# A mixture of experts on one core: nine instead of eight buffers for the experts' weights

## What is computed

```python
scores = jax.nn.sigmoid(ht @ w_router)              # 256 tokens x 64 experts
... # eight experts are chosen for each token, in four of eight groups
combine = ...                                       # weight of each chosen expert
a = jnp.einsum('td,edf->tef', hb, w_gate)           # 1024 -> 256, each expert
u = jnp.einsum('td,edf->tef', hb, w_up)             # 1024 -> 256
routed = jnp.einsum('tef,efd->td', silu(a) * u * combine[..., None], w_down)
shared = (silu(ht @ ws_gate) * (ht @ ws_up)) @ ws_down
x = x + gt2 * (routed + shared)                     # x is the residual
```

## Time and profile before

| | us |
|---|---|
| median of 3 runs | 1518.18 (1514.33 to 1518.4) |
| profiled execution, its own time | 1515.46 |
| its span, first to last instruction | 1513.6 |
| PE busy | 1451.0 (96%) |
| DVE busy | 985.3 (65%) |
| ACT busy | 792.3 (52%) |

### The profile page before, as it was taken

How to read it: one execution, slowest core, us unless ns; L and a number is a source line. 1 busy time by engine, 2 the same in 40 slices (tenths; PEclk the granted TensorE clock), 3 DMA queues, 4 the chain that set the end, 5 groups by cost and what they waited for, 6 DMA issues and landing times.

```text
span 1513.6 us, 39194 instructions
## 1 busy us (share of the span) xinstructions
PE 1451.0 (96%) x16093; PEld 1182.4 (78%) x16093; DVE 985.3 (65%) x1383; ACT 792.3 (52%) x1015; POOL 96.5 (6%) x57
## 2 busy tenths in 40 slices
PE   7999899999999999999999999899999999999998
PEld 6997767999999989999898999775555555555554
DVE  3597433367665457754645645678887787888786
ACT  5446226344333359634234445456767666767674
POOL 1200300002432000000310000000000000000000
PEclk9999999999999999999999999999999999999999
DMA  9667277455555535543123345379998999998994
GB/s 299 187 203 226 81 240 252 170 164 184 172 191 177 188 112 167 167 140 112 59 92 133 117 129 179 144 312 380 410 414 354 415 396 411 415 412 357 415 415 185
DMA packets 178599, 362.32 MB, mean 239 GB/s; under 512 B 9229, under 2 KB 137722, under 8 KB 161658
## 3 DMA queue, kind: packets, MB, share of 16 engines
q1 hardware_dynamic: 178426, 359.90, 65.5%
HBM read 355.03 MB, written 1.05 MB: 235 GB/s over the span
## 4 chain that ended last, share of the span: by engine, by line
PE 73%; DVE 6%; DMA 4%; ACT 4%; issue 2%; DVEq 1%; ACTq 0%; SPq 0%; POOLq 0%
PE psum L3395 11%; PE psum L372 9%; PE psum L373 8%; PE psum L376 8%; PE psum L3411 6%; DMA proj<-in_w_exp_up 4%; PE psum L3366 3%; PE psum L3448 3%; PE psum L569 3%; PE psum L704 3%; PE psum L505 2%; PE psum L506 2%; PE psum L507 2%; PE psum L547 2%; PE psum L1191 1%
## 5 line engine op out<-in xcount | busy, mean ns | idle before, releaser
L372 PE MATMUL psum<-proj_r 128*128 128x256 f32 x1392 | 341.6, 286 | 3.9 <-ACT proj_r L336 3.9
L373 PE MATMUL psum<-proj_r 128*128 128x256 f32 x1392 | 339.1, 284 | 0.0
L341 DVE TENSOR_TENSOR ring_r<-ring,proj_r 128x2048 fp32r<-128x2048 f32 x94 | 223.6, 2380 | 156.9 <-ACT proj_r L336 156.2
L2585 DVE COPY ring<-proj 128x1024 f32 x374 | 237.0, 686 | 91.8 <-PE psum L3395 53.5
L372 PEld LDWEIGHTS psum<-proj_r 128*128 128x128 f32 x1392 | 268.0, 193 | 8.3 <-issue 7.3
L373 PEld LDWEIGHTS psum<-proj_r 128*128 128x128 f32 x1392 | 268.1, 193 | 0.1
L336 ACT ACTIVATE proj_r<-ring 128x2048 fp32r<-128x2048 f32 x93 | 177.5, 1908 | 103.6 <-PE psum L376 93.1
L1919 ACT ACTIVATE ring<-proj 128x1024 f32 x186 | 188.9, 1051 | 6.6 <-issue 5.4
L376 PE MATMUL psum<-proj_r,ring_r 128*128 128x256 f32 x1392 | 181.3, 283 | 0.0
L376 PEld LDWEIGHTS psum<-proj_r,ring_r 128*128 128x128 f32 x1392 | 173.3, 192 | 0.1
L3395 PE MATMUL psum<-ring,u 128*32 128x256 f32 x1488 | 114.8, 386 | 3.2 <-DVE ring L2585 2.4
(11 more groups left out here) (570 smaller groups left out, 2621.5 us busy)
## 6 DMA issues: line engine op xcount, KB each, us to landing
ring<-in_w_in SPq DMA_DIRECT2D x65, 1024.0 KB, 5.3
proj<-in_w_exp_gate SPq DMA_DIRECT2D x64, 1024.0 KB, 9.4
proj<-in_w_exp_up SPq DMA_DIRECT2D x64, 1024.0 KB, 10.0
proj<-in_w_exp_down SPq DMA_DIRECT2D x64, 1024.0 KB, 8.2
ring<-in_w_ada SPq DMA_DIRECT2D x24, 1024.0 KB, 8.2
ring<-in_w_ffn_in SPq DMA_DIRECT2D x22, 1024.0 KB, 5.1
ring<-in_w_ffn_out SPq DMA_DIRECT2D x11, 1024.0 KB, 4.9
ring<-in_w_out SPq DMA_DIRECT2D x8, 1024.0 KB, 5.1
```

The lines of the kernel that those rows point to most:

```text
L341: dve.tensor_tensor(ring_r[:, at.slot, :], ring[:, at.slot, :], self.heads[at.buffer].bitcast(F32), ALU.subtract) \
L372: pe.matmul(dst, w, xh, start=start, stop=False, skip_group_check=True)
L373: pe.matmul(dst, w, xl, start=False, stop=False, skip_group_check=True)
L2585: ins = dve.tensor_copy(into_copy[k_half][j][:, kind * D:(kind + 1) * D], pieces[:, bass.ds((piece + kind) & 7, 1), of_half].rearrange("p ...
```

## The change

The ring gets a ninth buffer, `proj[:, 64:72]`. The copy that lay there (the second block's gate and up, lower half of the contraction) moves to `delta`. The residual's token rows, which lay in `delta`, are written to the output tensor in HBM before the piece d0 is issued (two DMAs of 512 KB), and read back into a ring buffer after the last piece (two DMAs again), for the last sums. The first copy into `delta` waits for the write. A piece now waits for the one nine places earlier, which is the same matrix of the expert three before.

```diff
-        pieces = proj[:, 0:64, :].rearrange("p (r k) n -> p r (k n)", r=8)
+        pieces = proj[:, 0:8 * PIECES, :].rearrange("p (r k) n -> p r (k n)", r=PIECES)
-        into_slots = [ring[:, 1, :], ring[:, 2, :], ring[:, 3, :], flat_of(proj[:, 64:72, :])]
+        into_slots = [ring[:, 1, :], ring[:, 2, :], ring[:, 3, :], flat_of(delta[:, :, :])]
+        h_back = pieces[:, (3 * EXPERTS + 1) % PIECES, :].rearrange("p (b d) -> p b d", b=TB)
...
+            def spill_h_tok():
+                sp.wait_ge(*reached("last_h_copied", 1))
+                for b in range(TB):
+                    sp.dma_start(out[0, b * P:(b + 1) * P], h_tok[:, b, :]).then_inc(sig("h_kept"), 16)
             for at, e, kind in piece_order:
-                if at - 8 in at_place:
-                    last, kind_before = at_place[at - 8]
-                    if at == 8:
+                if at == 5:
+                    spill_h_tok()
+                if at - PIECES in at_place:
+                    last, kind_before = at_place[at - PIECES]
+                    if at == PIECES:
...
-                dst = pieces[:, (at + 1) % 8, :]
+                dst = pieces[:, (at + 1) % PIECES, :]
...
+            sp.wait_ge(*reached("h_kept", 32))
+            last = EXPERTS - PIECES // 3
+            ended = sp.value_load(ends_of[:, last:last + 1], min_val=1, max_val=BLOCKS)
+            sp.wait_ge(*reached("into_copied", ended * 2 + (ended & 1)))
+            for b in range(TB):
+                sp.dma_start(h_back[:, b, :], out[0, b * P:(b + 1) * P]).then_inc(sig("h_returned"), 16)
...
-                                          pieces[:, bass.ds((piece + kind) & 7, 1), of_half].rearrange("p o n -> p (o n)"))
+                                          pieces[:, bass.ds((piece + kind) % PIECES, 1), of_half].rearrange("p o n -> p (o n)"))
...
             for k_half in range(2):
+                if k_half:
+                    dve.wait_ge(*reached("h_kept", 32))
                 copy_into(0, k_half, 1, by_block[1])
...
                 dve.wait_ge(*reached("moe_scaled", 3 + b))
-                dve.tensor_tensor(out_tok[:, b, 512:D], out_tok[:, b, 512:D], h_tok[:, b, 512:D], ALU.add).then_inc(sig(f"out_ready_{b}_1"), 1)
+                dve.wait_ge(*reached("h_returned", 32))
+                dve.tensor_tensor(out_tok[:, b, 512:D], out_tok[:, b, 512:D], h_back[:, b, 512:D], ALU.add).then_inc(sig(f"out_ready_{b}_1"), 1)
```

More of the change, by code:

```diff
@@ L39 @@
 SLOTS = 6
+PIECES = 9
 SLOT = 2048
@@ L145 @@
     "state_written": [("state_ready", 3), ("g_state_ready", 3)],
+    "tiles_moved": [("input_heads_moved", 16), ("input_rests_moved", 16), ("h_kept", 32), ("h_returned", 32)],
     "logits_made": [("att_scored", 2), ("d_scored", 8)],
@@ L1391, in _ @@
                     dst = dst.rearrange("p (f n) -> p f n", f=2)
-                sp.dma_start(dst, src).then_inc(sig(f"piece_loaded_{at % 8}"), 16)
+                sp.dma_start(dst, src).then_inc(sig(f"piece_loaded_{at % PIECES}"), 16)
+            sp.wait_ge(*reached("h_kept", 32))
[4 more added lines that the diff above has]
+                sp.dma_start(h_back[:, b, :], out[0, b * P:(b + 1) * P]).then_inc(sig("h_returned"), 16)
             for b, n in ((0, 0), (1, 0), (1, 1), (0, 1)):
@@ L1450, in _ @@
                 pool.tensor_tensor(u[:, pair, :], h[:, pair, :], spread(rs[:, :], 2), ALU.mult).then_inc(sig("pair_scaled"), 1)
-            loads_before = [0] * 8
+            loads_before = [0] * PIECES
             places_passed = 0
             for at, e, kind in piece_order:
-                loads_before[at % 8] += 1
-                pool.wait_ge(*reached(f"piece_loaded_{at % 8}", 16 * loads_before[at % 8]))
+                loads_before[at % PIECES] += 1
+                pool.wait_ge(*reached(f"piece_loaded_{at % PIECES}", 16 * loads_before[at % PIECES]))
                 pool.drain().then_inc(sig("pieces_in"), at + 1 - places_passed)
@@ L1460, in _ @@
                 pool.wait_ge(*reached("moe_scaled", b + 1))
-                pool.tensor_tensor(out_tok[:, b, 0:512], out_tok[:, b, 0:512], h_tok[:, b, 0:512], ALU.add).then_inc(sig(f"out_ready_{b}_0"), 1)
+                pool.wait_ge(*reached("h_returned", 32))
+                pool.tensor_tensor(out_tok[:, b, 0:512], out_tok[:, b, 0:512], h_back[:, b, 0:512], ALU.add).then_inc(sig(f"out_ready_{b}_0"), 1)
             st.end()
@@ L1916, in down_of_block @@
                     act.wait_ge(sig("pieces_in"), piece + 5)
-                    down_from.append(pieces[:, bass.ds((piece + 5) & 7, 1), :])
+                    down_from.append(pieces[:, bass.ds((piece + 5) % PIECES, 1), :])
                 at = slice(part * D, (part + 1) * D)
@@ L2594, in down_of_last @@
                 dve.wait_ge(sig("pieces_in"), piece + 5)
-                dve.tensor_copy(last_down[j], pieces[:, bass.ds((piece + 5) & 7, 1), :].rearrange("p o n -> p (o n)")).then_inc(sig("last_down_copied"), 1)
+                dve.tensor_copy(last_down[j], pieces[:, bass.ds((piece + 5) % PIECES, 1), :].rearrange("p o n -> p (o n)")).then_inc(sig("last_down_copied"), 1)
             choose(0)
```

## The result

| | before | changed |
|---|---|---|
| median of 6 runs, us | 1518.29 | 1508.2 (1503.95 to 1511.79) |
| profiled execution, us | 1515.46 | 1507.84 |
| its span | 1513.6 | 1506.0 |

The ratio is 0.9942, with a 95% interval of 0.9924 to 0.9961: 8.8 us less, 5.9 to 11.5 (the medians themselves are 10.1 us apart). The forecast was 3.6 us less, 1514.6 us, with a range that reached down to 1508.0 us; the time came out 0.2 us inside its edge, where the first rival stood.

What follows compares the result with a forecast made beforehand. PE was taken to set the time in the experts' stage, with late weights costing at most 12.8 us. Terms -2.5 - 0.4 - 0.7 = -3.6 us gave 1514.6 us against the median; range 1508 to 1519.5 us.

Steps and rivals of the forecast that it cites:

- the first rival: Falls of the clock at both places go or get shorter: -7 us up to the whole 12.8 us, 1505.4 to 1511 us; chance 0.22.
- Term 3: PE's wait at 1254.88 us and the low clock behind it stay: 0, bounds -2.9 - 3.4 us and 0.
- Term 1: Expert 20: d21 goes out within the stall, so u23 and all pieces behind it land one piece earlier: -2.5 us.
- The clock at 1173 us: PE would otherwise wait for u24, so it gains the pieces' 2.5 us, without adding the clock fall's 1.7 us.
- Term 2: The wait ahead of expert 20 goes, since the stream of pieces gets ahead at the start: -0.4 us.
- Term 4: Wait at 1490.03 us, expert 60: last up piece comes at least one place earlier: -0.7 us, bounds 0 and 1.14 us.
- Term 5: Residual's write at the start lands by 993.2 us, before the copy needing it; the stream's 2 to 3 us lead is cover: 0.
- Term 6: Residual's read back behind d63, more than 10 us ahead of POOL's first last sum: 0; without cover, up to 4.9 us.
- Term 7: Register remainder ahead of each copy, mostly done while the copy before runs: 0; decides from 0.34 us per remainder.

## Why the prediction was right, and where it fell short

The time lies in the stated range by 0.2 us only, and the gain is more than twice the forecast's. The forecast's own bounds (1.5 to 6 us) don't hold it; the range does, with some luck, since it takes in about half of the first rival's times, and that rival, at 0.22, is what happened: u33's lead grew by 2.4 us, one piece, and both falls of the clock are gone. Term by term the forecast was 2.5 + 0.4 + 0 + 0.7 = 3.6 us, and the two profiles have 2.8 + 0.4 + 5.2 + 0.4 = 8.8 us. The difference is term 3.

**Term 1 (-2.5 us, expert 20): right.** d21 and g23 went out as said (1152.92 and 1163.83 us), VectorE's wait came down by 1.95 us, and the stall put back costs 2.7 us in the stage. PE's wait moved in part to u24, as the short waits near 1181 us show.

**The clock at 1173 us: counted rightly.** I argued that TensorE would wait for u24 instead, so that the 1.7 us of the fall were already in the 2.5 us. The waits of 2.42, 0.30 and 0.48 us, 3.2 in sum, became four of 0.38 to 0.83 us, 2.15 in sum, and no fall came: 1.05 + 1.7 = 2.8 us, of which the clock is the larger part.

**Term 3 (0, the wait at 1254.88 us): this is the step that failed.** The sentence was: "Between expert 24 and expert 33 the queue is loaded, so u33 stays as far ahead as u24". It wasn't loaded at d29, where expert 28's third block held g28. Lead of u24 2.1 us, of u33 4.4 us; the wait of 2.90 us is 0.57 us, and the 6.8 us at half clock, 2.9 us of work, are gone: 5.2 us where the term has 0. The prediction had named just this as the sign that it is wrong, the wait near 1252 us gone. The stall put back at 28 alone brings 2.04 us of wait and one fall of 3.4 us back, some 3 of the 5.2 us; that the rest hangs on u32's wait for d28 is argued, not tested. I had given the whole of this as the bound of term 3 (2.9 + 3.4 us, of which the second part is 0.5 us too large, since the fall begins within the wait) and as the first rival, "if u33's lead grows by one piece more", with a chance of 0.22. The list of experts with three blocks stood in the text ahead of the prediction; for this stretch I looked for stalls only at the longest one.

**Term 2 (-0.4 us): the size came true, the reason isn't shown.** The wait ahead of expert 20 (0.43 us) is gone, but with d1 held back until the table is there as well, so the issue ahead of the table isn't what removes it. Whether the ninth buffer does or what is left of the lead at the start stays open.

**Term 4 (-0.7 us): within its bounds.** The wait near 1490 us went from 1.14 to 0.72 us, 0.4 us less; with the stalls at 46 and 60 put back it is 2.45 us. So without the ninth buffer's effect there it would have grown, I take it because TensorE, which gained time at experts 20 and 28, comes to this place earlier against the pieces.

**Term 5 (0, the write): right in sum, wrong in its times.** SP's timeline and the write's row in the DMA issues of 986.5 to 988 us:

```profile
986.84 1.12 SPq L1383 DMA_DIRECT2D out<-delta  x2
988.01 0.76 SPq L1404 DMA_DIRECT2D proj<-in_w_exp_down  x1
...
990.65 1.70 SPq L1404 DMA_DIRECT2D proj<-in_w_exp_down  x1
```

```profile
out<-delta SPq DMA_DIRECT2D x2, 512.0 KB, 5.0
```

d1 was issued at 990.65 us, not near 987: 1.9 us of this are the later start of this execution, the rest are SP's own issues, which take 0.5 to 1.2 us each here. The lead of 2 to 3 us that I had worked out is there: counted from the first piece's issue, d2 lands at +35.4 us instead of +37.7 us. With d1 held back until the table is there it lands at +35.5 us, so d1 needn't go out as early as it does; what differs from the kernel before is that it goes out before u2 has landed. There u2 landed at 995.8 us, and the queue was empty until d1's issue at 998.01 us. The write landed by 993 us at the latest (986.84 + 1.12 + 5.0), and the first copy into `delta` began at 998.63 us without a wait.

The Trainium skill (DMA: Bandwidth & Descriptors, Anatomy of one DMA) says that the completion of a write to HBM can take surprisingly long, in a section on DMAs that GpSimd issues; these went by SyncE's queue. No such delay shows here: the two writes of 512 KB landed 5.0 us after their issue with loads ahead of them, beside 4.9 us for a lone load of 1 MB.

**Term 6 (0, the read back): right.** The reads, issued at 1482.00 us, took 6.1 us to land behind the last pieces, and POOL's first last sum began at 1499.18 us, some 11 us later.

**Term 7 (0, the remainder): right.** 47 ns for a remainder, against the 0.34 us at which it would decide.

## What to carry to other kernels

Where a ring of buffers feeds the bounding engine, look at the issue times of all transfers for the places where the queue runs dry, not only at the longest: each such place adds its own lead, and a lead counts wherever the consumer is just in time. One more buffer helps as far as it lets a transfer pass such a stall; in this kernel its worth fell from 39 us for the eighth to 9 us for the ninth. Where one queue serves the ring in a fixed order, try the order in which the buffers come free first; here moving one of three kinds by one expert either way cost more than the ninth buffer gave.

## What the runs showed of the hardware

- Single waits of TensorE of 2.9 us and more in this stage, in all runs' profiles (2.90, 3.26, 3.46, 3.96, 4.08, 4.13 and longer), each came with a stretch at 1.2 GHz of 3.4 or 6.8 us, which began between 2.2 us before and 1.0 us after the wait's end. Of those between 1.8 and 2.8 us some did (1.88, 2.04, 2.20, 2.38, 2.42) and some did not (1.81, 1.86, 2.08, 2.17, 2.23, 2.24, 2.45, 2.73); shorter ones did not. The wait of 2.90 us cost 2.9 + 2.9 = 5.8 us in all, and the 0.57 us that is left of it costs 0.57 us.
- A remainder in a fused register group cost up to 47 ns on VectorE (94 ns for two, in the longest group).
- Two writes of 512 KB to HBM behind loads landed in 5.0 us, a lone load of 1 MB in 4.9 us.
